# Key updates and seven weight splits move from VectorE to GpSimd in a two-block transformer kernel

## What is computed

```python
S_t = diag(f_t) @ S_{t-1} + outer(k_t, v_t)
o_t = S_t.T @ q_t
```

## Time and profile before

| | before |
|---|---|
| median of 3 | 1202.27 us (1202.09 to 1202.72) |
| profiled execution | 1202.72 us, span 1200.2 us |
| granted TensorE clock, mean | 0.988 of full |
| TensorE busy | 1154.6 us, 96% |
| VectorE busy | 855.3 us, 71% |
| ScalarE busy | 521.5 us, 43% |
| GpSimd busy | 33.1 us, 3% |

### The profile page before, as it was taken

The page is one execution under the profiler, slowest core; times in us unless marked ns, Lnnn a source line. Parts: engine busy times, 40 slices in busy tenths (PEclk is TensorE's granted clock), DMA queues, the critical chain, the costliest instruction groups (busy, mean ns, idle before and its releaser), DMA issues.

```text
span 1200.2 us, 16339 instructions
## 1 busy us (share of the span) xinstructions
PE 1154.6 (96%) x7012; PEld 1023.0 (85%) x7012; DVE 855.3 (71%) x1007; ACT 521.5 (43%) x463; POOL 33.1 (3%) x53
## 2 busy tenths in 40 slices
PE   6999999999899999998999999999999999999996
PEld 5898898878699998876789998879976877999985
DVE  5689989975766677575657677478956857767755
ACT  5566555633444344444344344344322433434430
POOL 1000100000000000000000000000001000000000
PEclk8999999999999999998999999999999999999998
DMA  8763474447357768531356778548753563776761
GB/s 315 269 245 137 140 265 153 150 174 256 141 197 262 297 256 321 203 141 47 132 203 239 292 268 298 214 157 318 280 203 130 208 248 140 249 296 258 289 241 36
DMA packets 38647, 259.95 MB, mean 217 GB/s; under 512 B 4144, under 2 KB 6448, under 8 KB 7856
## 3 DMA queue, kind: packets, MB, share of 16 engines
q1 hardware_dynamic: 36960, 251.84, 57.4%
q0 software_dynamic: 1616, 7.08, 1.7%
HBM read 257.86 MB, written 1.05 MB: 216 GB/s over the span
## 4 chain that ended last, share of the span: by engine, by line
PE 75%; DVE 14%; DMA 4%; issue 3%; ACT 3%; POOL 1%; SPq 0%; DVEq 0%; POOLq 0%; ACTq 0%
PE pair L450 33%; PE pair L485 22%; PE pair L424 13%; DVE w_lo L1125 6%; DMA raw<-stream 3%; DVE hb L1173 2%; PE tp L568 2%; PE tp L503 1%; DMA mskf<-masks 1%; PE tp L730 1%; ACT w_hi L757 1%; PE tp L682 1%; DVE raw L1134 1%; PE tp L525 1%; POOL st L357 1%
## 5 line engine op out<-in xcount | busy, mean ns | idle before, releaser
L1125 DVE TENSOR_TENSOR w_lo<-raw,w_hi 128x2048 fp32r<-128x2048 f32 x182 | 415.3, 2289 | 104.8 <-ACT w_hi L757 104.7
L757 ACT ACTIVATE w_hi<-raw 128x2048 fp32r<-128x2048 f32 x182 | 344.5, 1911 | 212.2 <-DMA raw<-stream 125.9
L450 PE MATMUL pair<-ht_hi,w_lo 128*128 128x256 f32 x1184 | 336.1, 284 | 0.9 <-DVE w_lo L1125 0.9
L450 PE MATMUL pair<-ht_lo,w_hi 128*128 128x256 f32 x1184 | 335.0, 283 | 0.0
L450 PE MATMUL pair<-ht_hi,w_hi 128*128 128x256 f32 x1184 | 335.0, 283 | 0.0
L450 PEld LDWEIGHTS pair<-ht_hi,w_lo 128*128 128x128 f32 x1184 | 227.2, 192 | 1.2 <-DVE w_lo L1125 1.1
L450 PEld LDWEIGHTS pair<-ht_hi,w_hi 128*128 128x128 f32 x1184 | 227.2, 192 | 0.1
L450 PEld LDWEIGHTS pair<-ht_lo,w_hi 128*128 128x128 f32 x1184 | 227.2, 192 | 0.0
L424 PE MATMUL pair<-w_hi,ht_lo 128*128 128x512 f32 x384 | 156.3, 407 | 20.8 <-DVE w_lo L1125 12.3
L424 PE MATMUL pair<-w_lo,ht_hi 128*128 128x512 f32 x384 | 150.7, 392 | 0.0
L424 PE MATMUL pair<-w_hi,ht_hi 128*128 128x512 f32 x384 | 150.7, 392 | 0.0
(11 more groups left out here) (203 smaller groups left out, 1091.2 us busy)
## 6 DMA issues: line engine op xcount, KB each, us to landing
raw<-stream SPq DMA_DIRECT2D x238, 1024.0 KB, 5.0
xres<-x SPq DMA_DIRECT2D x2, 512.0 KB, 6.1
prow<-rows POOLq DMA_DIRECT2D x1, 1024.0 KB, 8.3
xres<-x POOLq DMA_DIRECT2D x2, 512.0 KB, 5.7
dt<-decay POOLq DMA_DIRECT2D x1, 1024.0 KB, 7.8
outT<-outb SPq DMA_DIRECT2D x4, 256.0 KB, 2.2
csr<-dft POOLq DMA_DIRECT2D x1, 768.0 KB, 4.6
crow<-rows POOLq DMA_DIRECT2D x1, 512.0 KB, 5.8
```

Of the source, the lines that this page charges most:

```text
L450: mm = pe.matmul(pair[use % 2][:, c, m * S:(m + 1) * S], a[:, k, m * P:(m + 1) * P], b[:, k, :], start=(k == 0 and n == 0), stop=(k == KT ...
L757: sc.activation(w_hi[:, w % WS, :], raw[:, n % RAW, :], ACT.Copy).then_inc(hi_done, 1)
L1125: v.tensor_tensor(w_lo[:, w % WS, :], raw[:, n % RAW, :], whi32[:, w % WS, :], ALU.subtract).then_inc(raw_done, 1)
```

## The change

Three things change.

1. The key updates of all levels go to GpSimd (`key_updates` in its program, one call per half). GpSimd starts a level when ScalarE has staged it and VectorE has done the totals of the level before. VectorE's totals wait for GpSimd's keys (`hg_kupd`).
2. Seven low-part splits go to GpSimd: the first chunk behind norm1, and the first two behind norm3, norm4 and norm5 (`NORMED`, `POOL_LO`, `split_los`). They stand in GpSimd's program between the powers of tile 0 and tile 1. GpSimd and VectorE both count in `raw_done`; `after_pool` makes VectorE wait where the item ahead is GpSimd's.
3. VectorE's loops over the levels are written out: the split comes ahead of the query update, and for most levels ahead of the scores; the totals of a level stand right behind its query update.

```diff
+NORMED = {"norm1": W0["wout"] + 3, "norm3": W0["fo"] + 3, "norm4": W0["down1"] + GROUPS - 1, "norm5": W0["ro"] + 7}
+POOL_LO = [w + 1 + j for name, w in NORMED.items() for j in range(1 if name == "norm1" else 2)]
...
+            def key_updates(half):
+
+                for lv in range(1, 8):
+                    h = 1 << (lv - 1)
+                    v = [a[:].rearrange("p a (b two h) -> p (a b) two h", two=2, h=h) for a in (kf, kb, tf, tb)]
+                    nb = HH * S // (2 * h)
+                    pool.wait_ge(hg_staged, 8 * half + lv + 1)
+                    if lv == 1:
+                        pool.wait_ge(hg_qupd, 8 * half + 1)
+                    else:
+                        pool.wait_ge(hg_tot, 6 * half + lv - 1)
+                    g.tensor_tensor(v[0][:, :, 0, :], v[0][:, :, 0, :], v[2][:, :, 1, 0:1].to_broadcast([P, nb, h]), ALU.mult)
+                    g.tensor_tensor(v[1][:, :, 1, :], v[1][:, :, 1, :], v[3][:, :, 0, 0:1].to_broadcast([P, nb, h]), ALU.mult).then_inc(hg_kupd, 1)
+
+            def split_los(w):
+
+                for c in [c for c in (w + 1, w + 2) if c in POOL_LO]:
+                    n = AT_RAW["w", c]
+                    pool.wait_ge(hi_done, c + 1)
+                    pool.wait_ge(raw_done, n)
+                    g.tensor_tensor(w_lo[:, c % WS, :], raw[:, n % RAW, :], w_hi[:, c % WS, :].bitcast(F32),
+                                    ALU.subtract).then_inc(raw_done, 1)
+
+            def norm_rsqrts(name):
+                rsqrt(RQ[name])
+                split_los(NORMED[name])
+                rsqrt(RQ[name] + 1)
...
             rsqrt(RQ["ln"], 2)
+            key_updates(0)
             for half in range(2):
...
             rsqrt(RQ["pva"], 2, 4)
+            key_updates(1)
             rsqrt(RQ["pvb"], 2, 4)
...
-            rsqrt(RQ["mix"], 4)
+            rsqrt(RQ["mix"], 2)
+            split_los(NORMED["norm1"])
+            rsqrt(RQ["mix"] + 2, 2)
...
-            rsqrt(RQ["norm3"], 2)
+            norm_rsqrts("norm3")
...
-            rsqrt(RQ["norm4"], 2)
+            norm_rsqrts("norm4")
             rsqrt(RQ["av"], 8)
-            rsqrt(RQ["norm5"], 2)
+            norm_rsqrts("norm5")
...
+            def after_pool(n):
+
+                if ORDER[n - 1] in [("w", w) for w in POOL_LO]:
+                    dve.wait_ge(raw_done, n)
+
             def split_lo(w):
                 if w >= NW:
                     return
                 n = AT_RAW["w", w]
+                if w in POOL_LO:
+                    return
+                after_pool(n)
                 at_least(dve, hi_done, w + 1)
...
+                if lv < 7:
+                    dve.wait_ge(hg_kupd, 7 * half + lv)
+                    dve.wait_ge(hg_qupd, 8 * half + lv + 1)
+                    v.tensor_tensor(fa[:, :, 0, 0:1], fa[:, :, 0, 0:1], fa[:, :, 1, 0:1], ALU.mult)
+                    v.tensor_tensor(fc[:, :, 0, 0:1], fc[:, :, 0, 0:1], fc[:, :, 1, 0:1], ALU.mult).then_inc(hg_tot, 1)
...
-            levels(0, "zi")
+            for lv in range(8):
+                if lv in (0, 1, 7):
+                    take_scores(0, lv)
+                    if lv == 0:
+                        gate_u()
+                tick(W0["zi"] + lv)
+                if lv not in (0, 1, 7):
+                    take_scores(0, lv)
+                if lv < 7:
+                    query_updates(0, lv + 1)
...
-            levels(1, "ga")
+            for lv in range(8):
+                if lv in (0, 7):
+                    take_scores(1, lv)
+                tick(W0["ga"] + lv)
+                if lv not in (0, 7):
+                    take_scores(1, lv)
+                if lv < 7:
+                    query_updates(1, lv + 1)
```

More of the change, by code:

```diff
@@ L1423, in _ @@
             head_gates(0, gate_positions)
[L1424 to L1432, removed]
-                        gate_u()
-                    tick(W0[name] + lv)
-            levels(0, "zi")
+            for lv in range(8):
+                if lv in (0, 1, 7):
+                    take_scores(0, lv)
+                    if lv == 0:
+                        gate_u()
+                tick(W0["zi"] + lv)
[3 more added lines that the diff above has]
+                    query_updates(0, lv + 1)
             tick(W0["qb"])
```

## The result

| | before | after |
|---|---|---|
| median | 1202.18 us (1201.14 to 1202.72, 4 runs) | 1223.18 us (1220.78 to 1225.64, 4 runs) |
| profiled execution, span | 1202.72 us, 1200.2 us | 1219.92 us, 1217.8 us |
| mean granted clock | 0.988 | 0.985 |

The changed kernel is slower: ratio 1.0178, 95% interval 1.0161 to 1.0196, +21.0 us. The forecast was 1213.0 us with a range up to 1222. The direction held, the size did not: the change costs almost twice the +10.8 us of the sum.

The account below looks back on a forecast made before the run. TensorE, busy 96% of the span, was taken as the bound, with time lost wherever VectorE's results come later. Terms 3.6 + 1.6 + 4.2 + 1.4 = +10.8 us gave 1213.0 us, range 1200 to 1222.

Parts of the forecast that it names:

- the sum: Whole kernel: levels 3.6 and 1.6, norm3 to norm5 4.2 and norm1 1.4 add up to +10.8 us.
- levels: Position-by-position levels: VectorE's totals wait for GpSimd's keys, delaying TensorE's scores, +3.6 us in half 0, +1.6 in half 1.
- norm1: Boundary norm1: GpSimd's split starts ahead of VectorE's xn and shuts it out, +1.4 us; otherwise -1.2.
- norm3 to norm5: Three boundaries: GpSimd's two splits hold up VectorE's ht_lo, so the residual sum comes later, +1.4 us each, 4.2 in all.
- The exclusion: GpSimd and VectorE operations with both inputs in SBUF don't run together; 1.2 us a key update, 4.6 a split.
- the two kb rows: Levels of the old trace: kb updates at 126.45 and 141.24 take 2.90 us instead of 0.69 beside a GpSimd operation.
- The rivals without exclusion: Levels and boundaries: GpSimd works beside VectorE, sum -9.3, 1193 us; chance 13%.
- with VectorE winning the turns: Boundaries and levels: exclusion holds but VectorE gets in first, +2 to +4 us, 1205 us; chance 15%.
- third rival: GpSimd slower on strided, broadcast keys or fp32r output, up to 1.8 us a key; sum +18, 1220 us; chance 17%.

Follow-up runs that it names:

- filled_short: Kernel before with the seven splits on GpSimd and 14 unused TensorE matmuls in its wait behind norm3, norm4 and norm5: 1209.73 us, +7.9 us.
- splits_only: Kernel before with only the seven splits moved to GpSimd, levels as before: 1215.97 us, +14.0 us.
- keys_only: Changed kernel with its seven splits back on VectorE, keys on GpSimd and new loops kept: 1209.62 us, +7.7 us against the kernel before.
- order_only: Changed kernel's loop order, but key updates on VectorE behind the query updates and no split moved: 1206.32 us, +4.4 us against the kernel before.
- norm1_only: Kernel before with only the one split behind norm1 moved to GpSimd: 1203.96 us, +1.8 us.
- best: Kernel before with the first split behind norm1, norm3, norm4 and norm5 on GpSimd, norm1's only after TensorE turned xn: 1197.64 us, ratio 0.9965.
- norm1_late: Kernel before with only norm1's split on GpSimd, started only when TensorE has turned xn: 1202.10 us, +0.2 us.

## Why the prediction was wrong

**Sum.** Predicted +10.8, measured +21.0: levels 7.7 for 5.2, norm1 1.8 for 1.4, and norm3 to norm5 together 14.0 - 1.8 = 12.2 for 4.2. The trace of the changed kernel has 7.1, 1.65 and 12.1.

**The exclusion** was read rightly from the two kb rows: 4.6 us a split (4.69), GpSimd getting in between two ht_lo (9.57 us for two splits without a break), VectorE's splits of 3.6 us where they meet a key. The rivals without exclusion and with VectorE winning the turns are out.

**The step that failed, norm3 to norm5.** The prediction says "Everything behind it, split w+3, norm, split w+4, hb, ht_lo, is as before, and TensorE's second row half waits for it now (606.45, 0.99 idle), so all of it passes". It followed VectorE's chain alone: on it the term was nearly right, +1.1 us from power to power for +1.4. But the late ht_lo also holds up TensorE's first row half, by 3.3 us more than before, and the turns of tile 1 stand behind most of that half in TensorE's order. What slack the turns had is used up by that: even with the clock up (filled_short) hb waits 0.72 us for them, and the boundary costs 2.0 us (from power to power 1.1 and then 0.8). With the clock down it costs more: against the 0.8 of filled_short the trace of splits_only has 1.5 more at each boundary, that of the changed kernel 2.4, 2.4 and 1.6, 6.3 in all. The price of a wait of TensorE in clock had no term in the sum at all; it is most of the 8.0 us missing here (6.1 by the medians of splits_only and filled_short). The trace of the kernel before had it to read: behind a wait of 3.40 us at 548.61 twelve matmuls follow each other at 0.43 us, as many as behind norm3 in the changed kernel.

**Levels, terms too small.** The walk through the levels gave the right places: TensorE idle ahead of the scores of level 2 and 3 in half 0 and once in half 1. Its sizes, with the 0.25 us added by which the changed kernel came earlier into the levels: +2.0 for 1.4 at level 2, +5.2 for 4.2 at level 3, then +4.7 for 3.6, and +2.4 for 1.6 in half 1. A key of levels 1 and 2 takes 1.52 us and not 1.2, and one of level 7 takes 1.06. That is the third rival's mechanism, halfway to its bound of 1.8 and in the first levels only. The lower clock during the scores of level 2 (3.44 instead of 2.02 us) costs nothing there, since TensorE then waits for VectorE anyway. The trace sums to 7.1, and so does that of keys_only (1.30 us behind at level 0, 8.41 at level 6 of half 1); the median's 7.7 is the same within its interval. And the prediction, which walked through the new order, did not name what order_only shows: more than half of this price is the order's, which puts a split of 2.2 us and once gate_u ahead of ScalarE's staging, and would be paid without GpSimd.

**Norm1** was right, in mechanism and in size: xn can be shut out (5.02 us), +1.65 us from power to power (10.68 to 12.33), +1.8 measured alone. It was taken by the order of the starts, with no row that showed it, so part of this is luck. The clock has a share here too that the forecast lacked: behind the 3.63 us that TensorE waits for xn the clock stayed up in the changed kernel and fell in norm1_only and in splits_only, whose traces have +1.90 and +2.97.

**Why the traces differ by less than the medians.** The spans of the two profiled executions differ by 17.6 us, the medians by 21.0. The stages that the change touches cost 7.1 + 1.65 + 12.1 = 20.8 us in the trace, as the medians do. The rest lies in stretches that the change leaves alone, and there the profiled execution of the kernel before was the slower one: by 1.4 us between 254 and 299, by 0.7 between 540 and 584, by 1.0 between 927 and 987, and by 0.25 ahead of the levels. In the first, TensorE waits equally long for gt_lo, before

```profile
260.55 0.80 PE L485 MATMUL pair<-w_hi,gt_lo 128*128 128x512 f32 x1 [1.57 <-DVE gt_lo L1191]
```

and after

```profile
267.40 0.50 PE L521 MATMUL pair<-w_hi,gt_lo 128*128 128x512 f32 x1 [1.57 <-DVE gt_lo L1236]
```

but seven slow matmuls follow before (granted clock 0.88 from 254 to 262 and 0.91 from 262 to 270) and none after (1.00). In the second, the same wait of 3.40 us is followed by twelve slow matmuls before and seven after; in the third, TensorE waits 1.03 us for a split before and not after. Single executions of one kernel differ in the same way: the 14 of the changed kernel run from 1219.92 to 1225.74 us, and the six with a mean granted clock of 0.981 or less are all above 1224.

**Left open.** No run here shows why the clock falls behind a wait in one execution and not in the next, nor what decides how long it then stays down.

## What to carry to other kernels

Before work goes to GpSimd, list which of VectorE's instructions stand beside it. Those with two SBUF inputs stop for all of an operation that reads (ht_lo), and so does a fast one with one SBUF input (xn, 1024 elements in 0.75 us), even for a fill. Those that read PSUM do not (hb took 2.64 us beside a split as before), so a split belongs beside hb and no second one behind it. When one engine gets later, walk TensorE's chain from the new wait as well, and price a wait that grows from half a microsecond to almost four with the slow matmuls behind it. And an order written by hand is a change of its own: move the work first and change the order separately.

## What was not expected of the hardware

- **Waits of the same length, different clocks.** Behind 3.8 us of idle time the clock fell at all three boundaries of the changed kernel. But behind the 1.57 us ahead of gt_lo it fell before and not after, and behind the same 3.14 us in norm1 it fell in best and not in norm1_late. The first matmul behind that wait, in best:

```profile
309.85 0.79 PE L459 MATMUL pair<-w_hi,ht_lo 128*128 128x512 f32 x1 [3.14 <-DVE ht_lo L1229]
```

and in norm1_late:

```profile
309.97 0.50 PE L459 MATMUL pair<-w_hi,ht_lo 128*128 128x512 f32 x1 [3.14 <-DVE ht_lo L1229]
```

In the window from 312 to 316 the granted clock is 0.51 in best and 1.00 in norm1_late, where it fell only from 318.77 on, behind a second wait of 1.94 us ahead of 317.64. So the length of the wait alone does not decide it. Behind norm3 the slow stretch lasted from 601.80 to 606.95 in the changed kernel and from 599.15 to 602.31 in splits_only, after waits of 3.81 and 3.82 us.

- **GpSimd's early keys are slower.** GpSimd's kf over the same 512 elements takes 1.52 us in the first two levels and 1.08 in the last; VectorE's kf updates averaged 685 ns over all levels. The size of the blocks is what differs between these levels; no run varied it alone.
- **Two records per filling matmul.** The 26 filling matmuls of 128 columns stand in the trace as 52 and took 5.96 us, 0.23 us each, about twice what I had reckoned.
